# Seven-product steps in four chunk pairs of the second up product of a two-block layer

## The chip, the cores and the metric

The kernel runs on one core of a Trainium2 chip. The metric is the device time of one execution in microseconds (us), the median of three runs. Beside it there is one profiled execution, with the time of every instruction on TensorE (PE), VectorE (DVE), ScalarE (ACT), GpSimd (POOL) and SyncE (SP), and of every DMA.

## The reference, cut to what matters

Two transformer blocks run over 256 tokens of width 2048, in float32. The change lies in the feed-forward part of the second block:

```python
h = rmsnorm_2(x, g_ffn[l])
u = causal_dwconv(h @ w_up[l], ffn_conv_w[l]) + ffn_conv_b[l]
gate, val = jnp.split(u, 2, axis=-1)
x = x + (jax.nn.silu(gate) * val) @ w_down[l]
```

`h` is 256 x 2048, `w_up` is 2048 x 11264, the depthwise convolution has three taps along the tokens, and `w_down` is 5632 x 2048. `h @ w_up` is "the second up product" here.

## The kernel before

**Chunks and granules.** Every large product is cut into chunks of 512 output columns, and a chunk into granules of 256 rows of the weight, streamed as 128 x 1024 numbers (512 KB). The second up product has 22 chunks (`up` 0 to 21) of 8 granules. A chunk has two PSUM banks, one for each half of the 256 tokens.

**Split operands.** The multiplication is done in a format with a shorter mantissa (fp32r), so each operand is split into a high part and a remainder, and each product is three: high by high, high by low, low by high. ACT casts a granule to its high part (`wh`, L938), DVE subtracts it from the raw numbers (`wl`, L1296), and PE does 12 matmuls of 128x128 by 128x512 for it (L1882 records them all).

**Slots.** `raw`, `wh` and `wl` have four slots each. SP fetches granule i once DVE is done with i-4, and ACT casts granule i once PE is done with i-4. So ACT and DVE can be at most three granules ahead of PE.

**The plan.** The order of the work on each engine is written out ahead, as rows: row s holds the cast and remainder of granule s, the fetch of s+4, the other work that `later(s, ...)` put there, in the order in which it was put, and PE's work on granule s-3. Every engine takes its part of the rows strictly in order, and semaphores tie the engines together; a row has no time of its own.

**After a chunk of the up product.** With `last` the chunk's last granule, `plan_up` starts at s = last+4 (a few rows later for chunks 1 and 2): `up_rows` (ACT L1216 and L1217 take the two banks to `ST`), `turn` one row later (two DVE transposes, L1413 and L1415, `ST` to `Y`), `leave` (POOL sends `Y` to memory), `bring` two rows behind the turn (POOL brings it back in another order, four DMAs into `Z`), `up_keep` at s+9 (ACT L1224 and L1225, `Z` to `FW`), and from s+10 the taps, a row apart: `up_first` (four on ACT, L1232), `up_second` (four on DVE, L1743), `up_third` (four on DVE, L1750 and L1753), `up_silu` (ACT L1236), `up_gated` (DVE L1757) and in the same row `act2_hi` (ACT L1240), and `act2_lo` (DVE L1761).

**Seven-product steps.** Three other products (`gated`, `out1`, `down`) treat two chunks side by side, and in some pairs of granules do two by two blocks with seven products in place of eight. Such a step takes the same granule of both chunks (slots i and i+1), in row i+1, and on PE in row i+4. Its parts, in order:

- ACT `base_hi` (L958, 128x1536), DVE `sums` (L1324, L1327, L1329), DVE `base_lo` (L1310, 128x1536), ACT `forms_hi` (L964, 128x2048), DVE `forms_lo` (L1333, 128x2048).
- PE `multiply_base`: 9 matmuls, which need `base_lo`. PE `multiply_forms`: 12 matmuls, which need `forms_lo`.
- Both raw slots are let go by `base_lo`, so the fetches of i+4 and i+5 start together.
- Four PSUM banks (`shared`) gather four of the products over all the pair's steps. Five rows behind the last step's i, ACT takes them to `tile_sums` (`shared_out`, four copies, L980), DVE adds them up in the two rows behind (`shared_sums` L1369 and L1371, `shared_last` L1376 and L1378), and `shared_bank` (DVE L1399, L1400, or L1404) adds them onto each chunk's own banks when the chunk is done.

In the second up product before the change there is no such step: chunk after chunk has 8 granules in the natural order, and the chunks alternate between banks 0, 1 and banks 2, 3.

Of the kernel before, what the change touches and what calls it, by code (L numbers as in the profile page):

```python
# [8 lines left out]
P = 128  # L9
# [88 lines left out]
def two_block_kernel(nc, t, out):  # L98
    with ExitStack() as ctx:
# [127 lines left out]
        tile_sums = tmp.rearrange("p (k c) -> p k c", k=4)  # L227
# [4 lines left out]
        xs_in, gated_in = (view(n, [P, 2, 4, P], o) for n, o in (("xs_in", o_a), ("gated_in", o_b + 32 * K)))  # L232
        xs_out, gated_out = (view(n, [P, 2, 4, P], o) for n, o in (("xs_out", o_a + 4 * K), ("gated_out", o_b + 36 * K)))
# [45 lines left out]
        seven_operand = {"gated": "ffn", "out1": "act1", "down": "act2"}  # L279
        side_by_side = {"gated": {}, "out1": {}, "down": {}}  # L280
# [68 lines left out]
        def turn(step, src, filled):  # L349
# [4 lines left out]
            later(step + 2, lambda: do("bring", n))  # L354
            return n
# [127 lines left out]
        def plan_gated(n):  # L483
            def after(s, chunk):
                chunk.drained = [("silu", n), ("gated", n)]
                if n // 2 in GATED_PAIRS:
                    do("shared_bank", n)
# [191 lines left out]
        for n in range(2, 22):  # L679
            last_up = product(t["w_up2"], "N", "ffn2", PAIRS16, ("up", n), plan_up(n), n)  # L680
# [4 lines left out]
        for q in range(2):  # L685
            cleared = ([("pool_out", 1)], [("x_split", 1, 1)]) if q == 0 else ([("shared_out", "down", 0)],) * 2
# [73 lines left out]
        def gated_at(n):  # L760

            return at("shared_bank", n) if n // 2 in GATED_PAIRS else product_of("gated", n)
# [54 lines left out]
        bases = {"gated": (gated_hi, gated_lo), "out1": (base_hi, base_lo), "down": (base_hi, base_lo)}  # L817
        x_places = {"gated": (gated_in, gated_out), "out1": (xs_in, xs_out), "down": (xs_in, xs_out)}
# [4 lines left out]
        def x_forms(unit):  # L823

            if unit.pair.stage == "gated":
                return [[x[:, unit.place, n] for x in (gated_xs_hi, gated_xs_lo)] for n in range(4)]
            k = 2 * unit.p
# [89 lines left out]
        def scalar(e):  # L917
# [8 lines left out]
            for name, args in phases:  # L926
# [32 lines left out]
                elif name == "forms_hi":  # L959
# [3 lines left out]
                    e.wait_ge(*at("sums", i))  # L963
                    e.copy(two_slots(wh, i), tile_sums.rearrange("p k c -> p (k c)")).then_inc(done[name], 1)  # L964
                elif name == "xs_hi":
                    stage, j = args
                    e.wait_ge(*at("xs_sum", stage, j))
                    if stage == "gated":
                        e.copy(gated_xs_hi[:], gated_out[:]).then_inc(done[name], 1)
# [3 lines left out]
                elif name == "shared_out":  # L973
# [5 lines left out]
                    for k, place in enumerate((0, 3, 2, 1)):  # L979
                        e.copy(tile_sums[:, place, :], ps[:, pair.shared + k, :]).then_inc(done[name], 1)  # L980
# [228 lines left out]
                elif name == "up_rows":  # L1209
# [5 lines left out]
                    e.wait_ge(*product_of("up", n))  # L1215
# [51 lines left out]
        def vector(e):  # L1267
# [22 lines left out]
            for name, args in phases:  # L1290
# [20 lines left out]
                elif name == "sums":  # L1311
                    i, = args
                    unit = seven[i]
                    b12, b11, b22, b21 = (two_slots(raw, i)[:, 512 * k:512 * k + 512] for k in range(4))
                    if unit is not unit.pair.units[0]:
                        e.wait_ge(*at("forms_lo", unit.former.i))
                    else:
# [12 lines left out]
                elif name == "forms_lo":  # L1330
                    i, = args
                    e.wait_ge(*at("forms_hi", i))
                    e.tensor_tensor(two_slots(wl, i), tile_sums.rearrange("p k c -> p (k c)"), two_slots(wh, i).bitcast(F32),  # L1333
                                    ALU.subtract).then_inc(done[name], 1)
                elif name == "xs_sum":
# [3 lines left out]
                    if j > 0:  # L1339
                        e.wait_ge(*at("xs_lo", stage, j - 1))  # L1340
                    elif stage != "gated":
# [11 lines left out]
                elif name == "xs_lo":  # L1353
                    stage, j = args
                    e.wait_ge(*at("xs_hi", stage, j))
                    if stage == "gated":
                        e.tensor_tensor(gated_xs_lo[:], gated_out[:], gated_xs_hi[:].bitcast(F32),
                                        ALU.subtract).then_inc(done[name], 1)
                        continue
                    hi, lo = (seven_tiles(x, stage, j)[:, :, 1] for x in operands[seven_operand[stage]])  # L1360
# [3 lines left out]
                elif name == "shared_sums":  # L1364

                    stage, q = args
                    p1, p7, p6, _ = (tile_sums[:, k, :] for k in range(4))
# [4 lines left out]
                elif name == "shared_last":  # L1372
                    stage, q = args
                    _, second, first, p5 = (tile_sums[:, k, :] for k in range(4))
# [4 lines left out]
                elif name == "shared_first":  # L1379
# [5 lines left out]
                    e.tensor_tensor(X[:, 0, n0], X[:, 0, n0], tile_sums[:, 0, :], ALU.add)  # L1385
                    e.tensor_tensor(X[:, 1, n0], X[:, 1, n0], tile_sums[:, 1, :], ALU.subtract).then_inc(done[name], 1)
                elif name == "shared_second":
# [4 lines left out]
                    e.tensor_tensor(X[:, :, n1], X[:, :, n1], tile_sums[:, 2:4, :], ALU.add).then_inc(done[name], 1)  # L1392
                elif name == "shared_bank":
                    n, = args
                    bank0, bank1 = banks(named["gated", n])
                    e.wait_ge(*product_of("gated", n))
                    if n % 2 == 0:
                        e.wait_ge(*at("shared_sums", "gated", n // 2))
                        e.tensor_tensor(bank0, bank0, tile_sums[:, 0, :], ALU.add)  # L1399
                        e.tensor_tensor(bank1, bank1, tile_sums[:, 1, :], ALU.subtract).then_inc(done[name], 1)  # L1400
                    else:
                        b = named["gated", n].bank
# [787 lines left out]
```

## Time and profile before

| | |
|---|---|
| median of three runs | 2405.98 us (2405.49 to 2408.77) |
| the profiled execution's own time | 2406.82 us |
| its span, first to last instruction | 2404.6 us |
| PE busy in the span | 2392.5 us (99%) |
| DVE busy | 1749.4 us (73%) |
| ACT busy | 1351.1 us (56%) |
| POOL busy | 190.6 us (8%) |
| mean DMA rate | 229 GB/s |

Matmuls overlap in the records: one is shown as 389 ns long, though the next starts 227 ns behind it. The seconds column of a merged row of DVE or ACT runs from the first start to the last end of the merged instructions; on both engines an instruction that waits for nothing starts a little before the one in front of it has ended.

### The profile page before, as it was taken

The numbers are of one execution on the slowest core, as the hardware profiler recorded it, in microseconds if no ns is written. First come the engines' busy times: TensorE is split into PE (matmuls) and PEld (weight loads), VectorE is DVE, ScalarE is ACT, GpSimd is POOL, SyncE is SP. The second block draws the span as 40 slices with busy tenths as digits, with TensorE's granted clock in tenths as the row PEclk, the third lists the DMA queues.
The fourth block names the chain that finished last, engine by engine and source line by source line (L and its number), as shares of the span: only waits on it lengthen the run. The fifth ranks groups of instructions, "written<-read, shape, count | busy, mean of one in ns | idle before, by whom it ended". The sixth has DMA issues, their size and how long they took to land.

```text
span 2404.6 us, 28035 instructions
## 1 busy us (share of the span) xinstructions
PE 2392.5 (99%) x10606; PEld 1980.5 (82%) x10606; DVE 1749.4 (73%) x2148; ACT 1351.1 (56%) x1649; POOL 190.6 (8%) x351
## 2 busy tenths in 40 slices
PE   9999999999999999999999999999999999999998
PEld 7888888888888888888888888888888888888887
DVE  7575555666778888889786865786577766678886
ACT  7554565445555555555555754544566666665554
POOL 0000000001000000000001100111111111110000
PEclk9999999999999999999999999999999999999999
DMA  8777655778866767776678777887788888886664
GB/s 275 225 221 232 193 192 184 215 238 246 259 218 221 229 222 222 226 235 229 195 227 274 246 235 220 256 245 236 235 244 249 241 244 241 242 241 206 219 215 160
DMA packets 155734, 550.06 MB, mean 229 GB/s; under 512 B 20176, under 2 KB 20688, under 8 KB 155216
## 3 DMA queue, kind: packets, MB, share of 16 engines
q1 hardware_dynamic: 131552, 470.91, 62.0%
q0 software_dynamic: 23472, 76.57, 11.6%
q8 instruction: 84, 1.38, 0.2%
q10 hardware_dynamic: 576, 0.79, 0.1%
q14 instruction: 50, 0.41, 0.1%
HBM read 507.82 MB, written 40.37 MB: 228 GB/s over the span
## 4 chain that ended last, share of the span: by engine, by line
PE 93%; DVE 4%; DMA 1%; ACT 1%; issue 1%; SPq 0%; ACTq 0%; DVEq 0%
PE ps L1882 92%; DVE wl L1296 1%; DMA raw<-in_w_ffn_in 1%; DMA raw<-in_w_in 0%; DMA raw<-in_w_ffn_out 0%; ACT wh L938 0%; DVE wl L1333 0%; DVE tmp L1324 0%; ACT wh L964 0%; PE ps L2020 0%; DVE tmp L1327 0%; ACT tmp L980 0%; DVE tmp L1329 0%; PE ps L2040 0%; DVE xs_in L1345 0%
## 5 line engine op out<-in xcount | busy, mean ns | idle before, releaser
L1296 DVE TENSOR_TENSOR wl<-raw,wh 128x1024 fp32r<-128x1024 f32 x786 | 954.3, 1221 | 590.1 <-ACT wh L938 589.2
L938 ACT CAST wh<-raw 128x1024 fp32r<-128x1024 f32 x786 | 820.3, 1049 | 731.4 <-PE ps L1882 702.4
L1882 PE MATMUL ps<-wh,x4g_hi 128*128 128x512 f32 x704 | 273.9, 389 | 0.0
L1882 PE MATMUL ps<-wl,x4g_hi 128*128 128x512 f32 x704 | 273.9, 389 | 0.0
L1882 PE MATMUL ps<-wh,x4g_lo 128*128 128x512 f32 x704 | 273.9, 389 | 0.0
L1882 PE MATMUL ps<-wh,h_hi 128*128 128x512 f32 x576 | 224.4, 392 | 2.0 <-DVE wl L1296 1.3
L1882 PE MATMUL ps<-wh,h_lo 128*128 128x512 f32 x576 | 223.0, 389 | 0.0
L1882 PE MATMUL ps<-wl,h_hi 128*128 128x512 f32 x576 | 222.8, 389 | 0.0
L1882 PE MATMUL ps<-wh,x1g_hi 128*128 128x512 f32 x564 | 219.4, 389 | 0.0
L1882 PE MATMUL ps<-wl,x1g_hi 128*128 128x512 f32 x564 | 219.4, 389 | 0.0
L1882 PE MATMUL ps<-wh,x1g_lo 128*128 128x512 f32 x564 | 219.4, 389 | 0.0
L1882 PE MATMUL ps<-wh,act_hi 128*128 128x512 f32 x560 | 218.0, 389 | 0.0
L1882 PE MATMUL ps<-wl,act_hi 128*128 128x512 f32 x560 | 217.9, 389 | 0.0
L1882 PE MATMUL ps<-wh,act_lo 128*128 128x512 f32 x560 | 217.9, 389 | 0.0
L1838 POOL DMA_DIRECT2D Z<-rows x268 | 146.2, 552 | 351.2 <-DMA rows<-Y 338.4
L1830 POOL DMA_DIRECT2D rows<-Y x67 | 37.5, 560 | 1607.0 <-DVE Y L1415 1607.0
L1882 PEld LDWEIGHTS ps<-wh,x4g_lo 128*128 128x128 f32 x704 | 132.1, 188 | 27.6
L1882 PEld LDWEIGHTS ps<-wh,x4g_hi 128*128 128x128 f32 x704 | 132.1, 188 | 27.4
L1882 PEld LDWEIGHTS ps<-wl,x4g_hi 128*128 128x128 f32 x704 | 132.1, 188 | 27.4
L964 ACT CAST wh<-tmp 128x2048 fp32r<-128x2048 f32 x44 | 84.3, 1915 | 89.4 <-DVE tmp L1329 84.4
L1882 PEld LDWEIGHTS ps<-wh,h_hi 128*128 128x128 f32 x576 | 108.0, 188 | 24.9 <-issue 2.1
L1882 PEld LDWEIGHTS ps<-wh,h_lo 128*128 128x128 f32 x576 | 108.1, 188 | 22.7
(384 smaller groups left out, 4067.0 us busy)
## 6 DMA issues: line engine op xcount, KB each, us to landing
raw<-in_w_in SPq DMA_DIRECT2D x196, 512.0 KB, 4.3
raw<-in_w_ffn_in SPq DMA_DIRECT2D x176, 512.0 KB, 4.3
raw<-in_w_up SPq DMA_DIRECT2D x176, 512.0 KB, 4.7
raw<-in_w_ffn_out SPq DMA_DIRECT2D x88, 512.0 KB, 4.3
raw<-in_w_down SPq DMA_DIRECT2D x88, 512.0 KB, 4.3
rows<-Y POOLq DMA_DIRECT2D x67, 512.0 KB, 5.3
Z<-rows POOLq DMA_DIRECT2D x268, 128.0 KB, 5.1
raw<-in_w_o SPq DMA_DIRECT2D x32, 512.0 KB, 4.4
```

Source lines behind the costliest of these rows:

```text
L938: e.copy(wh[:, i % RING, :], raw[:, slot, :]).then_inc(rounded, 1)
L964: e.copy(two_slots(wh, i), tile_sums.rearrange("p k c -> p (k c)")).then_inc(done[name], 1)
L1296: e.tensor_tensor(wl[:, r, :], raw[:, i % RAW, :], wh[:, r, :].bitcast(F32), ALU.subtract).then_inc(remainder, 1)
L1830: e.dma_start(rows_out[n % 2], Y[:]).then_inc(rows_left[n % 2], 16)
L1838: e.dma_start(ZA[32 * q:32 * q + 32], rows_out[n % 2, :, 256 * q:256 * q + 256].rearrange("(a i) e -> i a e", a=4)).then_inc(rows_back[n % ...
L1882: return e.matmul(dst, weights, x, start=start, stop=stop, skip_group_check=True)
```

## The change

Chunk pairs 1, 3, 5 and 7 of the second up product (chunks 2 and 3, 6 and 7, 10 and 11, 14 and 15) are treated side by side in banks 4 to 7, with two seven-product steps each; the other chunks stay as they were. The pair's 16 granules come in the order 0, 1, 4, 2, 6 of both chunks in turn, then 3, 5, 7 of the first and 3, 5, 7 of the second chunk; the steps are granules 4 and 6. With G the pair's first granule they are at i = G+4 and G+8, and `shared_out` is in row G+13. Banks 0 to 3 are the shared ones.

The sums for this product are made in a place of their own (`up_sums`), so that `tmp`, which holds `ST` and the taps, stays free for the taps. `xs_sum`, `xs_hi`, `xs_lo` make the sums of `h` once, in rows G to G+2 of pair 1.

The work behind each chunk is put in other rows by `up_late`, which gives four delays: of `up_rows`, of the bringing, of `up_keep` and the taps, and of the last four steps. For the two chunks in front of a pair (4 and 5, 8 and 9, 12 and 13): `up_rows` in rows G-3 and G+3, `turn` in G-2 and G+4, `bring` in G and G+13, `up_keep` in G+12 and G+20, the taps behind. For the two chunks of a pair: `shared_bank` in rows G+16 and G+21, `up_rows` in G+17 and G+23, `up_keep` in G+26 and G+32, and the second chunk's taps in G+33 to G+38. Counted from the first granule of the next side-by-side pair (there is none behind pair 7) these are rows 1 to 6, with `up_second` and `up_third` in rows 2 and 3 and `up_gated` and `act2_hi` in row 5. For chunks 0 and 1, in front of pair 1: `up_rows` in G+1 and G+4, `turn` in G+2 and G+5, `bring` in G+4 and G+13, `up_keep` in G+12 and G+20.

The diff, cut to its core:

```diff
-SEVEN = {"gated": (4, 6), "out1": (8, 10, 12, 14, 16, 18), "down": (8, 10, 12, 14, 16, 18)}
+SEVEN = {"gated": (4, 6), "up": (4, 6), "out1": (8, 10, 12, 14, 16, 18), "down": (8, 10, 12, 14, 16, 18)}
+UP_PAIRS = (1, 3, 5, 7)
+UP_ORDER = (0, 1, 4, 2, 6, 3, 5, 7)
...
+        up_hi = view("up_hi", [P, 3, 512], o_b + 28 * K, FR)
+        up_lo = view("up_lo", [P, 3, 512], o_b + 74 * K, FR)
+        up_sums = view("up_sums", [P, 4, 512], o_b + 80 * K)
...
+        def up_late(n):
+            if n < 2:
+                return ((0, 0, 2, 1), (1, 6, 7, 0))[n]
+            if n // 2 in UP_PAIRS:
+                return (1, 0, 0, 0) if n % 2 == 0 else (4, 0, 0, 0)
+            next_sums = n // 2 + 1 in UP_PAIRS
+            if n // 2 - 1 in UP_PAIRS and n % 2 == 0:
+                return 2, 0, 6 * next_sums, next_sums
+            return 0, 7 * next_sums, 8 * next_sums, 0
+
         def plan_up(n):
             def after(s, chunk):
                 chunk.drained = [("up_rows", n)]
-                s += (0, 4, 2)[n] if n < 3 else 0
+                rows_late, bring_late, take_late, silu_late = up_late(n)
+                if n // 2 in UP_PAIRS:
+                    later(s + n % 2 * 2, lambda: do("shared_bank", "up", n))
+                s += rows_late
 
                 def leave():
-                    rows_of["up", n] = turn(s + 1, ST, ("up_rows", n))
+                    rows_of["up", n] = turn(s + 1, ST, ("up_rows", n), bring_late)
...
-                later(s + 9, take)
+                later(s + 9 + take_late, take)
                 for i, name in enumerate(("up_first", "up_second", "up_third", "up_silu", "up_gated", "act2_hi", "act2_lo")):
-                    later(s + 10 + i - (i > 4), lambda name=name: do(name, n))
+                    later(s + take_late + 10 + i - (i > 4) + (i > 2) * silu_late, lambda name=name: do(name, n))
             return after
...
         product_pair(t["w_up2"], "ffn2", PAIRS16, [("up", 0), ("up", 1)], [plan_up(0), plan_up(1)])
-        for n in range(2, 22):
-            last_up = product(t["w_up2"], "N", "ffn2", PAIRS16, ("up", n), plan_up(n), n)
+        plan_x_sums("up", len(granules), 0)
+        for q in range(1, 11):
+            if q in UP_PAIRS:
+                cleared = [[("pool_out", 1)], [("x_split", 1, 1)]] if q == 1 else [[("up_rows", 2 * q - 4 + n)] for n in range(2)]
+                product_side_by_side(t["w_up2"], "up", q, 4, UP_ORDER, 5, [plan_up(2 * q), plan_up(2 * q + 1)], 0, cleared,
+                                     ("shared_out", "shared_sums", "shared_last"))
+                continue
+            for n in (2 * q, 2 * q + 1):
+                last_up = product(t["w_up2"], "N", "ffn2", PAIRS16, ("up", n), plan_up(n), n)
+                if q - 1 in UP_PAIRS:
+                    last_up.cleared = [("shared_out", "up", q - 1)]
```

## Rows read from the trace of the kernel before

**Rows 1.** The page: shares of the chain that ended last, by engine.

```profile
PE 93%; DVE 4%; DMA 1%; ACT 1%; issue 1%; SPq 0%; ACTq 0%; DVEq 0%
```

**Rows 2.** Windows: stretch and length, then each engine's busy time; PEclk; DMA share; GB/s.

```profile
1686.70:2165.40 478.70, 478.70 (x2113) 396.40 (x2112) 330.44 (x443) 297.26 (x393) 60.30 (x110) 1.00 0.82 242
948.40:1034.00 85.60, 85.15 (x374) 69.86 (x374) 72.27 (x75) 46.58 (x52) 5.76 (x11) 1.00 0.71 221
```

**Rows 3.** Timeline of PE, up product: start us, us, engine, line; two granules' first matmuls.

```profile
1904.31 0.39 PE L1882 MATMUL ps<-wh,x4g_hi 128*128 128x512 f32 x1
...
1907.03 0.39 PE L1882 MATMUL ps<-wh,x4g_hi 128*128 128x512 f32 x1
```

**Rows 4.** Timeline of ACT over one chunk of the up product.

```profile
1902.07 0.62 ACT L1240 CAST act_hi<-tmp 128x512 fp32r<-128x512 f32 x1 [1.89 <-DVE tmp L1757]
1902.59 1.04 ACT L938 CAST wh<-raw 128x1024 fp32r<-128x1024 f32 x1
1904.57 1.05 ACT L938 CAST wh<-raw 128x1024 fp32r<-128x1024 f32 x1 [0.93 <-PE ps L1882]
...
1907.29 1.05 ACT L938 CAST wh<-raw 128x1024 fp32r<-128x1024 f32 x1 [0.51 <-PE ps L1882]
1908.24 0.61 ACT L1224 COPY FW<-Z 128x512 f32<-128x512 f32 x1
1908.76 0.62 ACT L1225 COPY FW<-Z 128x512 f32<-128x512 f32 x1
...
1910.96 2.08 ACT L1232 ACTIVATE tmp<-FW,cst 128x256 f32<-128x256 f32 x4
1912.94 1.03 ACT L938 CAST wh<-raw 128x1024 fp32r<-128x1024 f32 x1
```

**Rows 5.** Timeline of DVE over the same chunk.

```profile
1901.35 0.68 DVE L1757 TENSOR_TENSOR tmp<-tmp 128x512 f32<-128x512 f32 x1
1903.67 1.23 DVE L1296 TENSOR_TENSOR wl<-raw,wh 128x1024 fp32r<-128x1024 f32 x1 [1.64 <-ACT wh L938]
...
1909.51 0.70 DVE L1413 STREAM_TRANSPOSE Y<-tmp 128x512 f32<-128x512 f32 x1
1910.14 0.67 DVE L1415 STREAM_TRANSPOSE Y<-tmp 128x512 f32<-128x512 f32 x1
...
1915.15 1.67 DVE L1743 SCALAR_TENSOR_TENSOR tmp<-FW,cst,tmp 128x255 f32<-128x255 f32 x4
1916.73 1.22 DVE L1296 TENSOR_TENSOR wl<-raw,wh 128x1024 fp32r<-128x1024 f32 x1
1917.87 1.26 DVE L1750 SCALAR_TENSOR_TENSOR tmp<-FW,cst,tmp 128x254 f32<-128x254 f32 x3
...
1919.44 1.22 DVE L1296 TENSOR_TENSOR wl<-raw,wh 128x1024 fp32r<-128x1024 f32 x1
```

**Rows 6.** Timeline of ACT, gated product: the taking of the shared banks.

```profile
923.40 2.03 ACT L980 COPY tmp<-ps 128x512 f32<-128x512 f32 x4
925.30 1.08 ACT L938 CAST wh<-raw 128x1024 fp32r<-128x1024 f32 x1
```

**Rows 7.** Timeline of DVE, gated product: shared sums, then parts of two steps.

```profile
927.55 0.68 DVE L1369 TENSOR_TENSOR tmp<-tmp 128x512 f32<-128x512 f32 x1
...
928.88 0.68 DVE L1574 TENSOR_TENSOR act_lo<-Z,act_hi 128x512 fp32r<-128x512 f32 x1
...
945.11 1.75 DVE L1310 TENSOR_TENSOR gated_lo<-raw,gated_hi 128x1536 fp32r<-128x1536 f32 x1
...
954.49 1.23 DVE L1324 TENSOR_TENSOR tmp<-raw 128x1024 f32<-128x1024 f32 x1 [2.68 <-DMA raw<-in_w_ffn_in]
...
957.09 1.75 DVE L1310 TENSOR_TENSOR gated_lo<-raw,gated_hi 128x1536 fp32r<-128x1536 f32 x1
959.23 2.29 DVE L1333 TENSOR_TENSOR wl<-tmp,wh 128x2048 fp32r<-128x2048 f32 x1 [0.39 <-ACT wh L964]
```

**Rows 8.** Timeline of PE, gated product: where it waited for the same step's forms.

```profile
961.57 0.50 PE L1882 MATMUL ps<-wh,gated_xs_hi 128*128 128x512 f32 x1 [0.26 <-DVE wl L1333]
961.91 0.39 PE L1882 MATMUL ps<-wl,gated_xs_hi 128*128 128x512 f32 x1
```

More of the change, by code:

```diff
@@ L347, in product_side_by_side, with turn @@
                 later(chunk.last + RING + late, lambda s=chunk.last + RING + late, n=n: afters[n](s, pair.chunks[n]))
-        def turn(step, src, filled):
+        def turn(step, src, filled, late=0):
             n = len(turns)
@@ L353, in turn @@
             do("leave", n)
-            later(step + 2, lambda: do("bring", n))
+            later(step + 2 + late, lambda: do("bring", n))
             return n
@@ L486, in after @@
                 if n // 2 in GATED_PAIRS:
-                    do("shared_bank", n)
+                    do("shared_bank", "gated", n)
                     later(s + 1, lambda: do("silu", n))
@@ L685, in two_block_kernel @@
         for q in range(2):
-            cleared = ([("pool_out", 1)], [("x_split", 1, 1)]) if q == 0 else ([("shared_out", "down", 0)],) * 2
+            cleared = ([("up_rows", 14)], [("up_rows", 15)]) if q == 0 else ([("shared_out", "down", 0)],) * 2
             product_side_by_side(t["w_down"], "down", q, (4, 0)[q], DOWN_ORDERS[q], DOWN_TAILS[q],
@@ L760, in gated_at, with up_at @@
         def gated_at(n):
-            return at("shared_bank", n) if n // 2 in GATED_PAIRS else product_of("gated", n)
+            return at("shared_bank", "gated", n) if n // 2 in GATED_PAIRS else product_of("gated", n)
+        def up_at(n):
+            return at("shared_bank", "up", n) if n // 2 in UP_PAIRS else product_of("up", n)
         def product_of(*key):
@@ L826, in x_forms @@
                 return [[x[:, unit.place, n] for x in (gated_xs_hi, gated_xs_lo)] for n in range(4)]
+            if unit.pair.stage == "up":
+                return [[x[:, n] for x in (up_xs_hi[:, unit.place], up_xs_lo[unit.place])] for n in range(4)]
             k = 2 * unit.p
@@ L963, in scalar @@
                     e.wait_ge(*at("sums", i))
+                    tile_sums = tile_sums_of[seven[i].pair.stage]
                     e.copy(two_slots(wh, i), tile_sums.rearrange("p k c -> p (k c)")).then_inc(done[name], 1)
@@ L967, in scalar @@
                     e.wait_ge(*at("xs_sum", stage, j))
-                    if stage == "gated":
-                        e.copy(gated_xs_hi[:], gated_out[:]).then_inc(done[name], 1)
+                    if stage in ("gated", "up"):
+                        x_hi = gated_xs_hi if stage == "gated" else up_xs_hi
+                        e.copy(x_hi[:], x_places[stage][1][:]).then_inc(done[name], 1)
                         continue
@@ L979, in scalar @@
                     for k, place in enumerate((0, 3, 2, 1)):
-                        e.copy(tile_sums[:, place, :], ps[:, pair.shared + k, :]).then_inc(done[name], 1)
+                        e.copy(tile_sums_of[stage][:, place, :], ps[:, pair.shared + k, :]).then_inc(done[name], 1)
                 elif name == "first_hi":
@@ L1316, in vector @@
                         e.wait_ge(*at("forms_lo", unit.former.i))
+                    elif unit.pair.stage == "up":
+                        if unit.pair.q > UP_PAIRS[0]:
+                            e.wait_ge(*at("shared_bank", "up", 2 * unit.pair.q - 3))
                     else:
@@ L1332, in vector @@
                     e.wait_ge(*at("forms_hi", i))
+                    tile_sums = tile_sums_of[seven[i].pair.stage]
                     e.tensor_tensor(two_slots(wl, i), tile_sums.rearrange("p k c -> p (k c)"), two_slots(wh, i).bitcast(F32),
@@ L1366, in vector @@
                     stage, q = args
-                    p1, p7, p6, _ = (tile_sums[:, k, :] for k in range(4))
+                    p1, p7, p6, _ = (tile_sums_of[stage][:, k, :] for k in range(4))
                     e.wait_ge(*at("shared_out", stage, q))
@@ L1373, in vector @@
                     stage, q = args
-                    _, second, first, p5 = (tile_sums[:, k, :] for k in range(4))
+                    _, second, first, p5 = (tile_sums_of[stage][:, k, :] for k in range(4))
                     e.wait_ge(*at("shared_sums", stage, q))
```

52 lines of the change are left out of this document (34 added, 18 removed).

## The prediction

> **What bounds the kernel now.** I read the chain of work that ended last first: 93% of it is PE [rows 1]. Then the windows, for the stretch of the second up product: PE is busy for all of its 478.70 us, DVE for 330.44 (69%), ACT for 297.26 [rows 2]. So before the change a matmul taken away here is worth its whole pitch, and DVE and ACT have room on the average. The second window is of the gated product, which already has what the change brings. There DVE is busy for 84%, and PE stood still for 0.45 us of 85.6. So seven-product steps need not starve PE, but they can.
>
> An average doesn't say whether a wait appears. ACT and DVE can be three granules ahead at most, so I follow the rows of one side-by-side pair, on the time axis of PE.
>
> **The axis.** Twelve matmuls take 2.72 us (1904.31 to 1907.03 [rows 3]), so one takes 0.2267. With P = 0 at the pair's first matmul, granules G to G+3 start at 0, 2.72, 5.44 and 8.16, the first step (21 matmuls, 4.76 us) at 10.88 with its forms at 12.92, G+6 at 15.64, the second step at 21.08 with its forms at 23.12, G+10 at 25.84, and G+16 six granules later. ACT's cast of granule i starts 0.26 us behind PE's end of i-4 (1904.57 against 1904.31 [rows 3, 4]), and PE can start 0.05 us behind the end of DVE's piece (959.23 + 2.29 = 961.52, PE at 961.57 [rows 7, 8]).
>
> **What goes.** Each step has 21 matmuls in place of 24; eight steps, 24 matmuls, 24 x 0.2267 = **-5.4 us**.
>
> **What comes, off the path.** Per step ACT has 1536 and 2048 columns in place of two casts, and DVE three sums and two remainders in place of two. `shared_out`, `shared_sums`, `shared_last` and `shared_bank` come to each pair, and the sums of `h` once. None of it costs as long as each piece of a granule is done when PE comes to it. Two places look late to me.
>
> **Place A: rows 2 to 9 of pairs 3, 5 and 7.** Row 3 holds the third tap of the chunk side by side two pairs before. In the trace DVE has the same pieces in the same rows. The taps of rows 2 and 3 follow the granules' remainders (1915.15, 1917.87), and the next remainder starts at 1919.44. PE starts the granule that stands for G at 1915.19, so DVE is free at 4.25 [rows 5]. Then, in DVE's order:
>
> - the turn of row 4, 1.30 us (1909.51 to 1910.81 [rows 5]): 5.55;
> - the step's sums from 5.58. From the sums' start to the end of `base_lo` it is 4.35 us (954.49 to 958.84), to the end of `forms_lo` 7.03 (to 961.52 [rows 7]): 9.93 and 12.61. PE needs them at 10.88 and 12.92, so the first step is in time by 0.95 and 0.31, less the 0.05;
> - row 5's `up_gated`, queued behind `forms_lo` on DVE, ends at 13.21 (12.61 + 0.68, begun 0.08 early). `act2_hi` of the same row waits for it on ACT, and the cast of G+6 is queued behind `act2_hi`. From the end of `up_gated` to the remainder's start is 1.64 us in the trace (1902.03 to 1903.67 [rows 4, 5]): 14.85, ended at 16.08, PE at 16.13. Due was 15.64, **0.5 us late**;
> - `act2_lo` 0.61 (a 128x512 piece takes 0.68 and starts 0.08 early), then G+7's remainder: 17.82. The second step's sums start at 17.85, its `forms_lo` ends at 24.88, PE at 24.93. Due was 23.12, **1.81 us late**, the 0.5 within it.
>
> After such a wait the next matmul but one comes 0.34 us later, not 0.23 (961.57 to 961.91 [rows 8]), so 0.11 more. Place A: 3 x 1.92 = **+5.8 us**. The landing isn't what is late: the fetches start at 9.93 and have till 17.85.
>
> Pair 1 has no taps in rows 2 to 5. Its first `base_lo` ends at about 9.5, and its turn lies behind the step. There the fetch decides, since the bringing of row 4 falls together with it. In the gated product such a case took 7.6 us (946.86 to 954.49 [rows 7]), which would make the forms 1.2 us late; it was also the case in which PE stood still. Without the bringing beside it there would be no wait. I take 0.1, with bounds of 0 and 1.2.
>
> The Trainium skill (DMA: Bandwidth & Descriptors, Anatomy of one DMA) fits a DMA as about 2.0 us plus its bytes over 436 GB/s, stated for the GpSimd path; for the two granules, 1 MB, an estimate by that page is 4.4 us, and pair 1 would never wait. The 7.6 us of the trace disagree, and they stay as the upper bound.
>
> **Place B: rows 12 to 16 of all four pairs.** Let R be the moment when ACT may cast again after the second step; both of its slots come free together, 0.26 us behind PE's end of it. ACT's queue from R is: cast 0.95 (1907.29 to 1908.24), `up_keep` 1.04 (twice 0.52), cast 0.95, `shared_out` 1.90 (923.40 to 925.30 [rows 6]), `up_first` 1.98 (1910.96 to 1912.94 [rows 4]). So the cast of G+14 starts at 6.82 and ends at 7.87, and DVE, idle since G+13's remainder, starts at 7.90. Its queue is: remainder 1.14, `shared_sums` 1.33 (927.55 to 928.88 [rows 7]), `up_second` 1.58, remainder 1.14, `shared_last` 1.33, `up_third` 1.57, those of the up product from [rows 5]. So G+16's remainder starts at 15.99, ends at 17.22, and PE can start at 17.27. PE is there at 6 x 2.72 - 0.26 = 16.06: **1.2 us late**. G+14 and G+15 are in time, by 1.5 and by 0.1. With the 0.11 of a restart and some hundredths at G+19, where `act2_hi` waits for `up_gated` again, it is 1.35 a pair: 4 x 1.35 = **+5.4 us**. Behind G+20 the queues are short (a remainder and at most 1.6 us a row), and DVE is back in step before the next pair.
>
> **The sum.** -5.4 + 5.8 + 0.1 + 5.4 = **+5.8 us**. The span goes from 2404.6 to 2410.4, and the execution's own time from 2406.82 to 2412.6. The median of the runs shown is 0.84 below that of the profiled one, so I predict **2411.8 us**. (0.2%, 4.8 us, is about what a measurement of this kernel can tell from no change.)
>
> **What is moved.** Bringing the second front chunk's rows in row 13 keeps four DMAs away from the fetches of rows 8 and 9; POOL's queue holds nothing else then, and `up_keep` takes them seven rows later. PE's opening of banks 0 to 3 waits for `up_rows` of row G+3, over at about 2.5 of 10.88. The change of banks behind a pair waits for `shared_out`, over at R+4.9 of 16. None of these costs. If the bringing were not hidden, it would come on top as in pair 1, up to 1.2 us a pair.
>
> **Rivals.**
>
> - *Everything is hidden.* The full -5.4: 2400.6. For it: DVE's sum over a pair with steps and one without is well under PE's time, and the gated product has DVE busy for 84% with almost no wait [rows 2]. Against it: the two queues above, each from measured pieces. It is this if DVE or ACT runs 1.8 us earlier in place A and 1.2 in place B than I have it.
> - *Only one place waits.* An order of the queues that I have misread, or slack that I have not counted, takes one of them away: +0.4 without A, +0.5 without B, 2406.4, not distinguishable.
> - *The backlog grows.* If the fetches of G+8 and G+9, or of G+12 and G+13, take the 7.6 us beside other transfers and DVE comes later still, about 1.2 us more in each pair: 2416 to 2417.
> - *The clock falls.* PE's short stops could lower its granted clock from 2.4 to 1.2 GHz. Twelve matmuls after each of some seven stops would cost 2.72 us more each, +19: 2431. The window with two stops in it shows 1.00 [rows 2]. The Trainium skill (TensorE: Matmul & The Clock Gate, HAM oscillation) warns of idle gaps that throttle the array; this case's trace, at 1.00 over its stops, gives that no support.
>
> **How the numbers follow.** My forecast has 0.52, of which 0.38 lies above +4.8 and 0.14 below, since +5.8 stands close to the bound. One place only: 0.24, no change. Hidden: 0.14, of which 0.11 beyond -0.2%, since even the full gain is only 0.226%. Growing backlog 0.09 and the clock 0.01, both slower. That is faster 0.11, same 0.41, slower 0.48. The range takes in one place only and reaches to the growing backlog: 2403.5 to 2417. The forecast's own range, from 0 or 1.2 in pair 1 and 0.4 us either way in each place, is 2408.5 to 2415.
>
> **What would show it.** In the after-trace PE's idle time before L1882 in the up product should be about 11 us, where it is 0 now. Its releasers should be `wl<-raw` at G+6, `up_lo` and `wl<-up_sums` at the second step of pairs 3, 5 and 7, and `wl<-raw` at G+16 of all four. The matmuls should be 24 fewer. ACT should stand still for some 3.0 us before `act2_hi` in row 5. I am wrong if PE never waits at G+16, if the second steps' sums start before 16 us on the pair's axis, or if the waits are for DMAs.

## The result, and the profile after

| | before | with the change |
|---|---|---|
| median of 6 runs each | 2406.51 us (2405.17 to 2409.2) | 2421.95 us (2418.15 to 2423.28) |
| profiled execution, its own time | 2406.82 | 2423.28 |
| its span | 2404.6 | 2421.5 |

The ratio is 1.0060, with a 95% interval of 1.0048 to 1.0073: the change costs 15.4 us. The direction is the forecast one. The size isn't: +5.8 us was forecast, and 2421.95 lies above the range of 2403.5 to 2417.

The page of the changed kernel, its busy times and its chain of waits (for the chain of before see [rows 1]):

```profile
PE 2394.0 (99%) x10582; PEld 1974.7 (82%) x10582; DVE 1802.8 (74%) x2206; ACT 1362.5 (56%) x1666; POOL 190.6 (8%) x351
...
PE 77%; DVE 13%; DMA 4%; ACT 4%; issue 2%; SPq 0%; ACTq 0%; DVEq 0%
```

The windows, for the up product, with the columns of [rows 2]:

```profile
1688.10:2181.70 493.60, 479.97 (x2087) 390.59 (x2087) 383.28 (x501) 308.49 (x410) 60.29 (x110) 1.00 0.78 235
```

The waits of PE in that stretch (releaser: us in all, how many, mean):

```profile
PE ps L1940 <- DVE up_lo L1354: 6.6, 5, 2.3
PE ps L1940 <- DVE wl L1340: 5.4, 6, 1.1
PE ps L1940 <- DVE wl L1382: 1.6, 6, 0.3
```

The product took 478.7 us before [rows 2]. This window leaves out its last two matmuls; to their end, at 2182.21, the product takes 494.1 us now, 15.4 longer, although it has 24 matmuls fewer. It also starts 1.4 us later, which isn't of the change: nothing ahead of it was edited, and in the profiles of the runs below, which share the code ahead of it, it starts anywhere from 1682.3 to 1690.3. PE's share of the chain falls from 93% to 77% and DVE takes 13%. DVE is busy for 78% of the stretch, so it isn't full. It is late at some places.

Where, the timeline of PE shows. I call a stop what the distance from one matmul's start to the next has above 0.227 us. Before there were none in this product; now they are, in us, restarts and slower matmuls with them (the first step is the one at 10.88 on the pair's axis):

| | pair 1 | pair 3 | pair 5 | pair 7 | sum | forecast |
|---|---|---|---|---|---|---|
| first step | 0 | 4.08 | 2.15 | 3.04 | 9.3 | 0 |
| G+6 and second step | 0.69 | 0.81 | 1.83 | 1.83 | 5.2 | 5.9 |
| G+16 | 1.35 | 1.35 | 1.36 | 1.36 | 5.4 | 5.4 |

That is 19.9 us in all; with -5.4 for the matmuls it makes +14.5 of the 15.4. (PE's idle time in the windows is less, 13.6 us: a matmul's record runs on for 0.16 us past the start of the next, and slower matmuls and restarts count as busy.) Place B came as forecast, and place A about so. The row that was not in the forecast is the first one, and it is the largest.

### The profile page after: what moved, and what is told of

Its sections match the earlier page's. It is cut to its first block, busy times and chain, and to the rows that moved or that the text cites. A ratio compares the mean times of both kernels' runs of the same rounds, so it can differ in the third digit from the quotient of the medians.

```text
span 2421.5 us, 28095 instructions
## 1 busy us (share of the span) xinstructions
PE 2394.0 (99%) x10582; PEld 1974.7 (82%) x10582; DVE 1802.8 (74%) x2206; ACT 1362.5 (56%) x1666; POOL 190.6 (8%) x351
## 4 chain that ended last, share of the span: by engine, by line
PE 77%; DVE 13%; DMA 4%; ACT 4%; issue 2%; SPq 0%; ACTq 0%; DVEq 0%
PE ps L1940 76%; DVE wl L1340 4%; DMA raw<-in_w_up 2%; DMA raw<-in_w_ffn_in 2%; ACT wh L980 2%; DVE wl L1382 1%; ACT wh L1007 1%; DVE tmp L1801 1%; DVE tmp L1372 1%; ACT tmp L1276 1%; DVE tmp L1808 1%; DMA raw<-in_w_in 1%; ACT tmp L1024 0%; DVE gated_lo L1354 0%; DVE up_sums L1372 0%
## 5 line engine op out<-in xcount | busy, mean ns | idle before, releaser
L1340 DVE TENSOR_TENSOR wl<-raw,wh 128x1024 fp32r<-128x1024 f32 x770 | 934.1, 1221 | 545.7 <-ACT wh L980 544.7
L980 ACT CAST wh<-raw 128x1024 fp32r<-128x1024 f32 x770 | 800.6, 1049 | 660.3 <-PE ps L1940 617.1
L1940 PE MATMUL ps<-wh,x4g_hi 128*128 128x512 f32 x648 | 252.7, 390 | 5.4 <-DVE wl L1340 5.4
L1940 PE MATMUL ps<-wh,x4g_lo 128*128 128x512 f32 x648 | 252.2, 389 | 0.0
L1940 PE MATMUL ps<-wl,x4g_hi 128*128 128x512 f32 x648 | 252.2, 389 | 0.0
L1940 PEld LDWEIGHTS ps<-wh,x4g_hi 128*128 128x128 f32 x648 | 121.6, 188 | 33.8 <-issue 6.1
L1940 PEld LDWEIGHTS ps<-wh,x4g_lo 128*128 128x128 f32 x648 | 121.6, 188 | 25.5
L1940 PEld LDWEIGHTS ps<-wl,x4g_hi 128*128 128x128 f32 x648 | 121.6, 188 | 24.7
```

Of the source, the lines that this page charges most:

```text
L980: e.copy(wh[:, i % RING, :], raw[:, slot, :]).then_inc(rounded, 1)
L1340: e.tensor_tensor(wl[:, r, :], raw[:, i % RAW, :], wh[:, r, :].bitcast(F32), ALU.subtract).then_inc(remainder, 1)
L1940: return e.matmul(dst, weights, x, start=start, stop=stop, skip_group_check=True)
```

## Place B, as it came

R, the moment when ACT may cast again, is 1941.95 in pair 5. The timeline of ACT from there:

```profile
1941.95 1.05 ACT L980 CAST wh<-raw 128x1024 fp32r<-128x1024 f32 x1 [3.59 <-PE ps L1940]
1942.90 0.61 ACT L1268 COPY FW<-Z 128x512 f32<-128x512 f32 x1
1943.42 0.62 ACT L1269 COPY FW<-Z 128x512 f32<-128x512 f32 x1
1943.94 1.05 ACT L980 CAST wh<-raw 128x1024 fp32r<-128x1024 f32 x1
1944.89 2.03 ACT L1024 COPY up_sums<-ps 128x512 f32<-128x512 f32 x4
1946.80 2.09 ACT L1276 ACTIVATE tmp<-FW,cst 128x256 f32<-128x256 f32 x4
1948.78 2.00 ACT L980 CAST wh<-raw 128x1024 fp32r<-128x1024 f32 x2
```

The remainders of G+14 and G+16 on DVE:

```profile
1949.86 1.22 DVE L1340 TENSOR_TENSOR wl<-raw,wh 128x1024 fp32r<-128x1024 f32 x1 [3.61 <-ACT wh L980]
...
1957.95 1.22 DVE L1340 TENSOR_TENSOR wl<-raw,wh 128x1024 fp32r<-128x1024 f32 x1
```

And PE at G+16:

```profile
1959.31 0.47 PE L1940 MATMUL ps<-wh,x4g_hi 128*128 128x512 f32 x1 [1.13 <-DVE wl L1340]
1959.62 0.40 PE L1940 MATMUL ps<-wl,x4g_hi 128*128 128x512 f32 x1
```

The cast of G+14 starts at R+6.83 (forecast R+6.82), its remainder at R+7.91 (R+7.90), G+16's remainder at R+16.00 (R+15.99). PE starts 0.14 us behind the remainder's end, where 0.05 was taken. The stop is 1.28 + 0.08 us in each pair, where 1.35 was forecast.

## The place that was not forecast

Pair 7. PE's G starts at 2002.98. The timeline of DVE:

```profile
2006.32 1.66 DVE L1801 SCALAR_TENSOR_TENSOR tmp<-FW,cst,tmp 128x255 f32<-128x255 f32 x4
2007.90 1.22 DVE L1340 TENSOR_TENSOR wl<-raw,wh 128x1024 fp32r<-128x1024 f32 x1
2009.03 1.27 DVE L1808 SCALAR_TENSOR_TENSOR tmp<-FW,cst,tmp 128x254 f32<-128x254 f32 x3
...
2010.61 0.71 DVE L1471 STREAM_TRANSPOSE Y<-tmp 128x512 f32<-128x512 f32 x1
...
2011.83 1.19 DVE L1372 TENSOR_TENSOR up_sums<-raw 128x1024 f32<-128x1024 f32 x1
```

The sums of the first step start at 8.85 on the pair's axis (2011.83 - 2002.98), where the forecast had 5.58. DVE's pieces and their order are those of the forecast; the third tap, which stands ahead of them, ends over 3 us late. So the backlog is older than the pair. ACT shows where it comes from (timeline of the changed kernel, from one `up_first` to the next):

```profile
1985.99 2.08 ACT L1276 ACTIVATE tmp<-FW,cst 128x256 f32<-128x256 f32 x4
1987.98 1.98 ACT L980 CAST wh<-raw 128x1024 fp32r<-128x1024 f32 x2
...
1994.60 0.64 ACT L1280 ACTIVATE tmp<-tmp 128x512 f32<-128x512 f32 x1 [2.54 <-DVE tmp L1811]
...
1998.66 0.62 ACT L1284 CAST act_hi<-tmp 128x512 fp32r<-128x512 f32 x1 [2.48 <-DVE tmp L1815]
1999.18 1.04 ACT L980 CAST wh<-raw 128x1024 fp32r<-128x1024 f32 x1
2000.13 0.62 ACT L1268 COPY FW<-Z 128x512 f32<-128x512 f32 x1
...
2001.18 1.04 ACT L980 CAST wh<-raw 128x1024 fp32r<-128x1024 f32 x1
2002.12 2.08 ACT L1276 ACTIVATE tmp<-FW,cst 128x256 f32<-128x256 f32 x4
```

From one `up_first` to the next it is 16.13 us, and in them ACT and DVE take turns: cast and remainder, second and third tap, `up_silu` that waits for DVE, `up_gated`, `act2_hi` that waits again, two casts and `up_keep`, the next `up_first`. Both engines stand idle in it (ACT for 2.54 and 2.48 us), but each waits for the other, and what is queued behind a waiting instruction waits too. Two chunks are six rows apart here, and six rows are 6 x 2.72 = 16.3 us. The chain gives back 0.2 us in them. What the change makes late at the end of a pair is therefore still late when the next pair's first step comes. Before the change there were chunks about six rows apart too (timeline of ACT of the kernel before, the taps of three chunks and ACT's waits between the last two):

```profile
1753.20 2.08 ACT L1232 ACTIVATE tmp<-FW,cst 128x256 f32<-128x256 f32 x4
...
1769.71 2.08 ACT L1232 ACTIVATE tmp<-FW,cst 128x256 f32<-128x256 f32 x4
...
1774.01 1.06 ACT L938 CAST wh<-raw 128x1024 fp32r<-128x1024 f32 x1 [1.28 <-PE ps L1882]
...
1776.72 1.05 ACT L938 CAST wh<-raw 128x1024 fp32r<-128x1024 f32 x1 [0.51 <-PE ps L1882]
...
1779.44 1.05 ACT L938 CAST wh<-raw 128x1024 fp32r<-128x1024 f32 x1 [0.51 <-PE ps L1882]
...
1785.86 2.08 ACT L1232 ACTIVATE tmp<-FW,cst 128x256 f32<-128x256 f32 x4
```

The distances are 16.51 and 16.15 us, but they aren't the length of the chain: ACT waits for PE for 2.3 us within the second, so PE's pace sets it and nothing had to be caught up. In the changed kernel no wait between the two `up_first` is for PE, so there the 16.13 us are the chain's own.

My theory, after this reading, was that the 9.3 us are place B's lateness, carried by that chain. The rivals were that place A makes its own lateness in the pair (too much work on DVE in its rows), that `act2_hi`'s wait in row 5 is the trouble, and that the fetches are.

## The experiments

All edits are against the changed kernel. Ratios are to the kernel before, in the same call, whose medians were 2406.01, 2406.47 and 2406.63 us. "Stops" is the sum of the table above, read from each one's profile; less 5.4 us for the matmuls it should give the difference in time. It does within 1.3 us, but for the runs with pairs 1 and 5 (2.1) and with `up_silu` a row later (2.2), and for the last row, a single execution (4.8), in whose profile the product starts 3.6 us later than before.

| | median us | ratio, 95% | stops us |
|---|---|---|---|
| one pair | 2407.23 | 1.0002 [0.9993, 1.0012] | 2.1 |
| pairs 1 and 5 | 2409.01 | 1.0009 [0.9999, 1.0018] | 3.6 |
| front taps two rows earlier | 2407.18 | 1.0004 [0.9994, 1.0013] | 6.1 |
| `act2_hi` later for the pair's second chunk | 2417.44 | 1.0042 [1.0027, 1.0057] | 15.6 |
| both of these | 2404.03 | 0.9992 [0.9983, 1.0] | 2.1 |
| and chunk 0's bringing later | 2403.37 | 0.9987 [0.9979, 0.9996] | 3.1 |
| `up_silu` a row later | 2431.03 | 1.0107 [1.0091, 1.0122] | 27.8 |
| all, and `up_silu` later for three chunks | 2401.57 | 0.9982 [0.9973, 0.9991] | 1.2 |
| `act2_hi` later for all chunks | 2407.53 | 1.0008 [0.9999, 1.0017] | 6.9 |
| first front chunk alone two rows earlier | 2407.87 | 1.0003 [0.9993, 1.0012] | 6.8 |
| all without the bringing | 2402.32 | 0.9982 [0.9973, 0.999] | 0.5 |
| the changed kernel once more | 2424.16 | (one run) | 18.2 |

In the first two, with fewer steps, fewer matmuls go: 6 and 12 in place of 24. In both, PE's wait for `shared_bank` before a pair's shared banks are opened also names the pair with steps ahead of it, in place of the pair two before.

**One pair alone, and pairs far apart.** Does a pair stop PE when no pair with steps is ahead of it?

```diff
-UP_PAIRS = (1, 3, 5, 7)
+UP_PAIRS = (1,)
```

> Steps in pair 1 alone. Carried lateness (ACT and DVE, once late at G+16, stay late through the next chunks because the taps come every six rows): a single pair has only its own stops, 2.1 us in the changed kernel's trace, against 1.4 us saved; +0.7 us on before, and PE never stops behind the pair's own G+16. Rival, each pair costs its share by itself (a quarter of the 15.4 us measured): +3.9 us. Rival, the cost lies in the moved rows of the front chunks alone: as for the first, stops only there.

```diff
-UP_PAIRS = (1, 3, 5, 7)
+UP_PAIRS = (1, 5)
...
-            if n // 2 - 1 in UP_PAIRS and n % 2 == 0:
+            if n % 2 == 0 and (n // 2 - 1 in UP_PAIRS or next_sums):
```

(The second edit gives chunk 8, which now has no pair with steps ahead of it, the delays of a first front chunk.)

> Steps in pairs 1 and 5 alone, so that six chunks, and not two, lie between them. Carried lateness: pair 5 starts with ACT and DVE in step and with no taps of a side-by-side chunk in its rows 1 to 6; its first step is in time, and it stops PE about as pair 1 does, 1.4 to 2.1 us; in all +0.8 to +1.5 us on before. Rival, a later pair costs what it costs wherever it stands (5.4 us of stops in pair 5 of the changed kernel): +4.7 us, and a wait of over 1 us before the first step's base.

With one pair, PE stops at the second step (0.52), at G+15 (0.25) and at G+16 (1.26 + 0.08), and nowhere behind. In the second run pair 5, with three pairs without steps ahead of it, has both its steps and G+6 in time and stops at its G+16 alone (timeline of PE):

```profile
1950.95 0.47 PE L1940 MATMUL ps<-wh,x4g_hi 128*128 128x512 f32 x1 [1.13 <-DVE wl L1340]
```

So place B comes with each pair that has steps, by itself. The first steps' stops need a pair with steps not far ahead. More this run can't tell: with pair 3 free of steps its chunks' taps come earlier too, so place A's taps were gone from pair 5's rows along with the backlog. Its median is 3.0 us above before, between what I expected (0.8 to 1.5) and the rival's 4.7; by its profile the product itself takes 1.1 us more (479.8 against 478.7 us) and starts 2.2 us later, so most of the difference isn't in the product.

**Take away place B.** Two rows earlier, the front chunks' `up_keep` and taps no longer fall together with `shared_out` and the shared sums.

```diff
-                return ((0, 0, 2, 1), (1, 6, 7, 0))[n]
+                return ((0, 0, 0, 1), (1, 6, 5, 0))[n]
...
-                return 2, 0, 6 * next_sums, next_sums
-            return 0, 7 * next_sums, 8 * next_sums, 0
+                return 2, 0, 4 * next_sums, next_sums
+            return 0, 7 * next_sums, 6 * next_sums, 0
```

> All four pairs, but up_keep and the taps of both front chunks two rows earlier (rows G+10 and G+18), so that the first taps on ACT no longer stand behind shared_out. Carried lateness: the stops at G+16 go (4 x 1.37 = 5.5 us), and with them most of the 1.5 to 2.4 us before the first steps of pairs 3, 5 and 7 and the slow matmuls of pair 3; only the prediction's place A stays, up to 1.9 a pair: +1 to +4 us on before. Rival, the first step of a pair is late for reasons of its own: only the 5.5 us go, +10 us.

Then the same for the first front chunk alone (`(0, 0, 0, 1), (1, 6, 7, 0)` and `4 * next_sums`, the other line as it was):

> The changed kernel with up_keep and the taps of the first front chunk alone two rows earlier (G+10); the second front chunk's stay at G+20. If shared_out in front of the taps on ACT makes G+16 late and everything behind inherits it: the stops at G+16 go, and the first steps of pairs 3, 5 and 7 come in time or at most 1 us late, +1 to +3 us on before. Rival, the later taps (six rows apart from G+21 on) make the lateness of the first steps themselves: only 5.5 us go, +8 to +10 us.

The stops at G+16 are gone in both, and with them nearly all of the first steps': 0.3 us in pair 3 of the one, 0.5 in pair 3 and 0.2 in pair 7 of the other, none in pair 5 of either. What is left is place A as it was forecast, and 0.8 us in pair 1. The waits of PE, taps two rows earlier:

```profile
PE ps L1940 <- DVE wl L1382: 1.1, 4, 0.3
PE ps L1940 <- DVE up_lo L1354: 1.0, 3, 0.3
PE ps L1940 <- DVE wl L1340: 0.9, 3, 0.4
```

Pairs 5 and 7 stop for 1.6 us each there, at G+6 and the second step, where 1.92 was forecast; before their first steps, `base_lo` ends 1.07 us and `forms_lo` 0.43 us early (forecast 0.95 and 0.31). So my count of place A was good for a DVE that comes in time.

**Leave place B and shorten the chain.** This is the other way round. `act2_hi` and `act2_lo` one row later, so that no cast stands behind a wait for `up_gated`:

```diff
-                    later(s + take_late + 10 + i - (i > 4) + (i > 2) * silu_late, lambda name=name: do(name, n))
+                    later(s + take_late + 10 + i - (i > 4) * (n // 2 not in UP_PAIRS or n % 2 == 0) + (i > 2) * silu_late, lambda name=name: do(name, n))
```

for the second chunk of each pair with steps,

> All four pairs, but act2_hi and act2_lo of a pair's second chunk one row later (G+38 and G+39), so that row 6's cast doesn't stand behind act2_hi, which waits for up_gated behind forms_lo. If that queue is the cause of the stop at G+6: this stop goes (0.6 + 0.1 us in pairs 5 and 7) and the second step comes earlier; the stops before the first step and at G+16 stay. In all 1.5 to 3 us less than the changed kernel, +12 to +14 us on before. Rival, DVE is simply busy there and ACT's wait is cover: no change, +15.4 us.

and `- (i > 5)` in place of `- (i > 4)` (one row later for all chunks, `act2_lo` as it was):

> The changed kernel, its stops at G+16 left in, with act2_hi one row later for every chunk of the up product, so that no cast stands behind it while it waits for up_gated. DVE's work and its order stay the same but for the waits. If the lateness is carried by the chain from one up_first to the next (16.13 us in the trace for six rows of 16.3), that chain loses a cast of 0.95: the distance falls towards 15.2 while the engines are late, they catch up about 1 us a chunk, and the stops before the first steps of pairs 3, 5 and 7 (2.4, 1.6 and 2.4 us) fall under 1 us; with the stops at G+6 gone too: +8 to +11 us on before. Rival, DVE's work is the bound: the distance stays at 16.1, only the stops at G+6 go, +12 us as with the pair's second chunk alone.

The first took away the stops at G+6 and left the first steps' (2.03, 1.60, 1.60, and slower matmuls behind the first of them) and those at G+16: 2417.44, 11.4 us above before, where 12 to 14 were expected. `act2_hi`'s wait of row 5 is the cause of G+6, as forecast, and not of the first steps. The second came 0.9 us above before, where I expected 8 to 11. The timeline of ACT, first taps of three chunks in it:

```profile
1955.56 2.08 ACT L1276 ACTIVATE tmp<-FW,cst 128x256 f32<-128x256 f32 x4
...
1970.83 2.07 ACT L1276 ACTIVATE tmp<-FW,cst 128x256 f32<-128x256 f32 x4
...
1986.23 2.08 ACT L1276 ACTIVATE tmp<-FW,cst 128x256 f32<-128x256 f32 x4
```

and its waits of PE:

```profile
PE ps L1940 <- DVE wl L1340: 4.5, 4, 1.1
PE ps L1940 <- DVE wl L1382: 0.5, 2, 0.3
```

The chain is 15.27 and 15.40 us long in place of 16.13, so it gives back 0.9 to 1.05 in six rows. All four stops at G+16 are there, unchanged (1.28 + 0.08). The first steps are in time, but for 0.7 us in pair 5, and so are G+6 and the second steps of pairs 3, 5 and 7, but for 0.2 us in pair 5. No work was taken off an engine. This is the run that settles it: with place B's lateness kept and only the chain shortened, what was carried is gone.

**Lengthen the chain.** `up_silu` and what follows a row later for a pair's own chunks, so that ACT wouldn't stand before it.

```diff
-                return (1, 0, 0, 0) if n % 2 == 0 else (4, 0, 0, 0)
+                return (1, 0, 0, 1) if n % 2 == 0 else (4, 0, 0, 1)
```

> The changed kernel with nothing but up_silu and what follows it one row later for the chunks of a pair; the stops at G+16 stay in it. Carried lateness by taking turns: ACT's casts of rows G+30 and G+36 no longer wait behind up_silu for DVE's third taps, the two engines come back into step between the pairs, and the 1.5 to 2.4 us before the first steps of pairs 3, 5 and 7 shrink to under 1; +8 to +11 us on before. Rival, DVE has simply too much work in these rows: the moved waits change nothing, +15.4 us within 1.

I was wrong: 2431.03, the slowest of all. The timeline of ACT, two first taps:

```profile
1893.11 2.08 ACT L1276 ACTIVATE tmp<-FW,cst 128x256 f32<-128x256 f32 x4
...
1911.41 2.08 ACT L1276 ACTIVATE tmp<-FW,cst 128x256 f32<-128x256 f32 x4 [1.90 <-DVE act_lo L1819]
```

The distance grew to 18.30 us, because `act2_lo` now stands in the row of the next `up_first`, which waits for it (they share `tmp`). The first steps' stops grew to 3.74, 3.73 and 4.23 us. It is the theory's other side: two us more in the chain, and 1.3 to 2.2 more before each first step.

**Towards a version that gains.** Taps two rows earlier and `act2_hi` later, together:

> Both edits of before in one: the front chunks' up_keep and taps two rows earlier, and act2_hi and act2_lo of a pair's second chunk one row later. If the second step of pairs 3, 5 and 7 is late because row 6's cast stands behind act2_hi, its sums now start some 1.7 us earlier (at about 16.1 on the pair's axis and not 17.9), and PE's stops in those pairs go from 1.6 to 1.9 us each to under 0.7; with pair 1's of 0.8 some 2 to 3 us of stops are left against 5.4 saved: 2403 to 2404, 2.5 to 3.5 us under before. Rival, the second step waits for its fetches (landing 5 to 7.5 us behind the first base_lo): half of the stops or more stay, and the releaser is a DMA: no change on before.

with chunk 0's bringing four rows later (`(0, 4, 0, 1)`), away from the fetches of pair 1's second step:

> The run with both edits, and the bringing of chunk 0's rows four rows later (G+8 in place of G+4), so that it doesn't run beside the fetches of pair 1's second step. If that is what makes the second step of pair 1 late (its granules landed 7 to 9 us behind base_lo), they land in about 5 us and pair 1's stop of 0.5 to 0.8 us goes. Rival, the landing is late for another cause (the stores and fetches of the step itself): no change in pair 1.

with `up_silu` later only for the second chunk of pairs 1, 3 and 5, behind whose taps the next ones are more than six rows away (`(4, 0, 0, n // 2 + 2 in UP_PAIRS)`):

> The run with the later bringing, and up_silu and what follows it one row later for the second chunk of pairs 1, 3 and 5. If the order of the queues is all that PE still waits for, up_gated of row 6 now lies behind row 6's remainder, no step has a stop of over 0.3 us, and nearly all of the 5.4 us shows: 2401 to 2402. Rival, the second step's fetches or DVE's own work are the limit by now: as the run without this edit.

and that without the bringing:

> The best run so far without its later bringing of chunk 0's rows. If that bringing, now in row G+8 of pair 1, is what makes up_keep and pair 3's first step late there (0.9 us of stops), these go and pair 1's stop of 0.5 comes back: 0.3 to 0.7 us better, 2401, not to be told apart by the clock but in the stops. Rival, pair 3's stop has nothing to do with it: 0.5 us worse.

The first leaves 0.5 us a pair, at `forms_lo` of the second step. The later bringing takes away pair 1's stop (the second fetch lands after 4.93 us, not 6.97) and puts 1.5 us in and ahead of pair 3, so it gains nothing that the times can tell. The last has one stop left, 0.43 + 0.11 us (timeline of PE):

```profile
1750.27 0.50 PE L1940 MATMUL ps<-wh,up_xs_hi 128*128 128x512 f32 x1 [0.27 <-DVE wl L1382]
```

and in the windows PE is busy for 485.73 of 486.00 us there:

```profile
1684.00:2170.00 486.00, 485.73 (x2143) 401.82 (x2143) 393.30 (x515) 321.48 (x425) 61.06 (x111) 1.00 0.80 244
```

It takes 2402.32 us, ratio 0.9982 [0.9973, 0.999], 4.3 us faster than before and, by the medians, 19.6 faster than the change. The one with the bringing (2401.57, the same ratio) can't be told from it. Both keep the 24 matmuls fewer and differ from the change in the rows alone.

**The changed kernel once more**, for what varies by itself:

> The changed kernel once more, for one look. The stops at G+16 (1.28 us and the slower restart) and those before the first steps come again within 0.1 us where the order of the queues makes them. The nine or so matmuls of pair 3 at 427 ns, which followed its longest stop, come again if the stop's length decides, and not if it is a matter of when it falls.

18.2 us of stops: at G+16 1.28 each as before, the first steps 1.69, 1.57 and 1.60, G+6 0.6 in all three pairs, and no slow matmuls. So place B repeats to 0.01 us, and the first steps' stops of pairs 3 and 7 vary by some 0.8 us. The difference goes with the fetches. The timeline of ACT in the first profile of the changed kernel, behind pairs 1 and 5:

```profile
1790.72 1.05 ACT L980 CAST wh<-raw 128x1024 fp32r<-128x1024 f32 x1 [2.13 <-DMA raw<-in_w_up]
...
1979.58 1.05 ACT L980 CAST wh<-raw 128x1024 fp32r<-128x1024 f32 x1 [1.34 <-DMA raw<-in_w_up]
```

Two granules landed late; in the second profile these waits are 0.64 us and none. `act2_hi` later for the pair's second chunk has such a wait of 1.42 us behind pair 1, and there pair 3's stop is 2.03 us and the others' 1.60. So about 1.6 us of each first step's stop is the chain's, and what is above it goes with a late landing; why these land late, no run shows.

## Why the prediction was wrong in its size

- **What goes, -5.4: right.** The best version gets 4.3 us of it, with 0.5 us of stops left.
- **Place B, +5.4: right**, 5.4 measured, each step of ACT's and DVE's queues to 0.01 or 0.02 us, and its stops vanish when the taps leave those rows.
- **Place A, +5.8: right in its cause, 4.5 measured.** Pairs 5 and 7 stop for 1.83 us each at G+6 and the second step, where 1.92 was forecast (0.61 + 0.11 at G+6, forecast 0.5). Pair 3 stops for 0.81 only. Its slower matmuls had moved PE back and left DVE that time; in the second profile of the changed kernel, where they are missing, pair 3 stops for 1.85.
- **Pair 1, +0.1: 0.7 measured**, within its bounds of 0 and 1.2. The bringing beside the fetches was the cause, as the upper bound had it.
- **The step that failed** is the sentence behind place B: "Behind G+20 the queues are short (a remainder and at most 1.6 us a row), and DVE is back in step before the next pair." With it falls place A's start, "DVE is free at 4.25", which was read from the trace of before, where DVE has no backlog. I counted the work of a row (1.14 + 1.6 us, within its 2.72) and not the chain of the two engines over six rows, 16.13 us of 16.3. It could have been added up from the pieces that I had. From one `up_first` to the next: `up_first` 1.98, cast 1.08, then on DVE remainder 1.14, `up_second` 1.58, remainder 1.14, `up_third` 1.57, remainder 1.14, a turn 1.22, remainder 1.14, `up_gated` 0.72, and on ACT `act2_hi` 0.52, cast 0.95, `up_keep` 1.04, cast 0.95, each from [rows 4, 5]: 16.2 us. The missing term is 9.3 us: 7.7 of late first steps with their restarts, and 1.6 of slower matmuls.
- **The rivals.** The growing backlog was the nearest, in what it does, but it named late fetches as its cause, and its 1.2 us a pair was too little. No wait of PE in this product ends with a DMA. Late landings made pair 1's stop and go with some 0.8 us each of the stops of pairs 3 and 7, in one of the changed kernel's two profiles; the rest is the chain's. "Everything is hidden" and "only one place waits" are out by the traces. (Without place A the prediction's own terms make +0.1, not the +0.4 that it gives, and 0.4 us a place around its forecast is 2408.9 to 2415.7, not 2408.5 to 2415; neither touches the range.) The clock had 0.01 and an amount of +19 us; what happened is 1.6 us in one pair, in one of the two profiles.
- **What would show it.** The named releasers came, but for `wl<-raw` at G+6 of pair 3, and ACT stood still for 2.96 us before `act2_hi` in pair 7 (forecast 3.0). But `up_lo` ends waits at the first steps too, and some 11 us of waits were named, where 19.9 us of stops came (13.6 by the profile's idle time).

What is carried isn't the 1.3 us by which PE stopped at G+16, since that moved PE too. It is the lead: how long before PE's first matmul of a granule DVE was done with its remainder. At the first granule of pair 7, in the changed kernel (timelines of DVE and PE),

```profile
2000.26 1.23 DVE L1340 TENSOR_TENSOR wl<-raw,wh 128x1024 fp32r<-128x1024 f32 x1 [1.64 <-ACT wh L980]
...
2002.98 0.39 PE L1940 MATMUL ps<-wh,x4g_hi 128*128 128x512 f32 x1
```

and with the taps two rows earlier:

```profile
1985.59 1.23 DVE L1340 TENSOR_TENSOR wl<-raw,wh 128x1024 fp32r<-128x1024 f32 x1 [1.64 <-ACT wh L980]
...
1991.66 0.39 PE L1940 MATMUL ps<-wh,x4g_hi 128*128 128x512 f32 x1
```

The lead is 1.5 us in the one and 4.8 in the other. Followed from pair 5 to pair 7, in us, by the same subtraction:

| | at G+22 of pair 5 | at G of pair 7 | stop before pair 7's first step |
|---|---|---|---|
| changed kernel | 2.50 | 1.49 | 2.43 |
| once more | 2.47 | 2.31 | 1.61 |
| first front chunk alone two rows earlier | 5.40 | 4.33 | 0 |
| `act2_hi` later for all chunks | 3.42 | 5.59 | 0 |

So place B costs 2.9 us of lead, and the chain keeps it from coming back for the ten rows behind; the shorter chain wins 2.2 us of it back. With the taps two rows earlier `base_lo` ends 1.07 us early, and PE needs 0.15 of that behind it. That leaves 0.92 us to spare at a lead of 4.84: a lead of 2.31 makes 4.84 - 2.31 - 0.92 = 1.61 us, and one of 1.49 makes 2.43, which are the two stops measured. With one pair alone the lead is still 2.4 us where pair 3's G would be, 16 rows behind the stop at G+16.

## What to carry to other kernels

When two engines with queues in order take turns on one chain, compare the length of the chain with the rows that it has, not each engine's work with its time; 78% of busy time on DVE hid a chain that took 16.13 us of its 16.3. Add the chain up from its pieces, or read it as the distance between two instances, but only where neither engine waits for a third within it. A lateness found at one place has to be followed until a row shows that it is gone. Where a delay is to be put into such a chain, look at both ends: an instruction that is moved off one wait can land in front of the next tap.

## What the chip showed that I had not expected

**The clock behind a stop.** After the 2.44 us stop before pair 3's first step, seven matmuls ran some 0.43 us apart in place of 0.227; after one of 2.42 us in pair 7 none did. Windows of the changed kernel behind the two stops:

```profile
1833.50:1837.00 3.50, 3.50 (x11) 2.67 (x10) 2.48 (x2) 0.99 (x2) 0.00 (x0) 0.53 0.87 300
...
2016.60:2020.00 3.40, 3.13 (x14) 2.27 (x13) 2.81 (x2) 0.56 (x2) 0.00 (x0) 1.00 0.82 280
```

0.53 is the lower level, 1.2 GHz, in nearly all of the first window; 1.00 is the upper, 2.4 GHz. With `up_silu` later, stops of 3.74, 3.73 and 4.23 us gave 1.00, 0.57 and 0.50 behind them; with `act2_hi` later for the pairs' second chunks, one of 2.03 us was followed by seven matmuls 0.43 us apart and two of 1.60 weren't. So the length of the last stop alone doesn't say it, and it cost 1.6 to 2.3 us each time, not the 2.72 that I had put. The Trainium skill (TensorE: Matmul & The Clock Gate, HAM oscillation) warns of idle gaps that throttle the array, a rule that my prediction found no support for in the trace of before. Three of these traces show the lower clock behind such a gap, and none of them behind every one.

**A restart costs more than the wait.** Behind a stop the next matmul comes 0.31 to 0.34 us later, not 0.227, in each of the stops above (1959.31 to 1959.62). Some 0.1 us for each, 1.8 us over the 19 stops of this product.
